# A recurrent and attention block on one core: a blocked inverse in four quadrants, and fewer small operations in differential attention

## The reference, cut to what matters

```
sa = S_{t-1} a_t
S_t = S_{t-1} diag(w_t) + sa b_t^T + v_t k_t^T ;  y_t = S_t r_t
```

## Time and profile before

| | us |
|---|---|
| median of 3 runs (lowest, highest) | 3494.92 (3494.77, 3496.0) |
| the profiled execution | 3495.8 |
| its span on the core | 3494.0 |
| PE busy | 3296.9 (94%) |
| DVE busy | 2061.9 (59%) |
| ACT busy | 1019.0 (29%) |
| POOL busy | 1679.5 (48%) |

### The profile page before, as it was taken

The page is one execution under the profiler, slowest core; times in us unless marked ns, Lnnn a source line. Parts: engine busy times, 40 slices in busy tenths (PEclk is TensorE's granted clock), DMA queues, the critical chain, the costliest instruction groups (busy, mean ns, idle before and its releaser), DMA issues.

```text
span 3494.0 us, 54483 instructions
## 1 busy us (share of the span) xinstructions
PE 3296.9 (94%) x20334; PEld 2615.5 (75%) x20334; DVE 2061.9 (59%) x2829; ACT 1019.0 (29%) x1866; POOL 1679.5 (48%) x1323
## 2 busy tenths in 40 slices
PE   7988999999999999989899899999989999999999
PEld 4766777777888888657778788887657677788887
DVE  4647777874566555541745575557551645576556
ACT  2152322222121112551435231113462435231112
POOL 3423222222657664225264566665326363666665
PEclk9999999999999999999999999999999999999999
DMA  5431111111323332112021233332102121223332
GB/s 204 166 123 45 38 32 38 31 38 43 115 70 96 96 97 72 37 43 91 31 89 53 83 92 96 96 97 67 54 25 91 49 79 49 85 85 97 94 94 95
DMA packets 71664, 268.48 MB, mean 77 GB/s; under 512 B 7840, under 2 KB 7968, under 8 KB 68384
## 3 DMA queue, kind: packets, MB, share of 16 engines
q1 hardware_dynamic: 69152, 260.73, 23.8%
q10 hardware_dynamic: 2304, 4.83, 0.4%
HBM read 263.44 MB, written 2.10 MB: 76 GB/s over the span
## 4 chain that ended last, share of the span: by engine, by line
PE 74%; DVE 19%; ACT 3%; issue 2%; DMA 1%; DVEq 0%; POOL 0%; SPq 0%; ACTq 0%; POOLq 0%
PE psum_a L574 10%; PE psum_a L577 10%; PE psum_a L578 10%; PE psum_d L574 5%; PE psum_d L577 4%; PE psum_d L578 4%; PE psum_d L637 4%; PE psum_d L1195 3%; PE psum_a L729 2%; PE psum_a L600 2%; PE psum_d L832 2%; PE psum_a L604 2%; PE psum_a L603 2%; DVE arena L2672 1%; PE psum_a L759 1%
## 5 line engine op out<-in xcount | busy, mean ns | idle before, releaser
L3274 POOL TENSOR_TENSOR w_lo<-raw,w_hi 128x1024 fp32r<-128x1024 f32 x440 | 1119.4, 2544 | 36.7
L3270 POOL TENSOR_TENSOR mark<-mark 128x1 f32<-128x1 f32 x438 | 105.5, 241 | 1738.4 <-PE psum_a L574 899.3
L574 PE MATMUL psum_a<-h_hi,w_hi 128*128 128x512 f32 x1712 | 675.2, 394 | 0.0
L577 PE MATMUL psum_a<-h_lo,w_hi 128*128 128x512 f32 x1712 | 667.4, 390 | 0.0
L578 PE MATMUL psum_a<-h_hi,w_lo 128*128 128x512 f32 x1712 | 667.4, 390 | 0.0
L3271 POOL TENSOR_SCALAR w_hi<-raw 128x1024 fp32r<-128x1024 f32 x440 | 471.2, 1071 | 33.7 <-DMA raw<-in_weights 33.7
L574 PEld LDWEIGHTS psum_a<-h_hi,w_hi 128*128 128x128 f32 x1712 | 322.1, 188 | 77.8 <-issue 11.2
L578 PEld LDWEIGHTS psum_a<-h_hi,w_lo 128*128 128x128 f32 x1712 | 322.0, 188 | 67.7
L577 PEld LDWEIGHTS psum_a<-h_lo,w_hi 128*128 128x128 f32 x1712 | 322.0, 188 | 67.4 <-issue 1.9
L574 PE MATMUL psum_d<-split,w_hi 128*128 128x512 f32 x848 | 331.2, 391 | 9.5 <-DVE x L3021 6.7
L577 PE MATMUL psum_d<-split,w_hi 128*128 128x512 f32 x848 | 330.0, 389 | 0.0
(11 more groups left out here) (393 smaller groups left out, 5775.5 us busy)
## 6 DMA issues: line engine op xcount, KB each, us to landing
raw<-in_weights SPq DMA_DIRECT2D x440, 512.0 KB, 3.6
plain<-in_ada SPq DMA_DIRECT2D x20, 1024.0 KB, 7.3
arena<-in_ada SPq DMA_DIRECT2D x4, 1024.0 KB, 17.4
x<-in_x SPq DMA_DIRECT2D x1, 2048.0 KB, 12.7
x<-in_x ACTq DMA_DIRECT2D x1, 2048.0 KB, 10.4
out<-x SPq DMA_DIRECT2D x8, 256.0 KB, 3.8
arena<-in_pe ACTq DMA_DIRECT2D x2, 512.0 KB, 3.6
const<-in_const ACTq DMA_DIRECT2D x1, 906.0 KB, 9.2
```

Of the source, the lines that this page charges most:

```text
L574: m = pe.eng.matmul(dst, wh, hi(t), start=t == 0, stop=False)
L577: pe.eng.matmul(dst, wh, lo(t), start=False, stop=False)
L3270: eng.tensor_tensor(b.mark[:, 1:2], b.mark[:, 0:1], b.mark[:, 0:1], ALU.add)
L3274: eng.tensor_tensor(lo, b.raw[:, s], hi.bitcast(F32), ALU.subtract).then_inc(sig["w_ready"], 1)
```

## The change

In the inverse, the third product and TC go. TN is transposed in each level by four PE transposes, which ACT copies to a new buffer, R_TW; the second product takes that. The first and second products (`products`) address all four pairs of row half and column half, where before two were used, and their results come in two banks by row half, 256 columns each, so that DVE's mask and its add are two operations of 256 columns each. The result of the first product lies swapped between halves, and the second swaps it back. After level 5 one more product with the identity (`diagonal`) gives the transposed blocks, which DVE copies to R_TF. R_TF holds the whole 128x128 transposed inverse, its unused quarter set to zero for j < 2, so `second` is one product of 128 rows for each head in place of two parts.

In the order: `second` stands ahead of the level's second product, on PE alone; `dve_rwkv_normed` stands ahead of level 1; the first maps of level 5 are made and masked behind that level's second product and its adds.

In differential attention the two negatives are one operation behind the second unit's maximum, so ACT waits once for a pair; the two reciprocals are one; and the sum of squares is taken by ACT, one step later.

```diff
         self.R_Z, self.R_TN = (ar(a).rearrange("p (u t) -> p u t", u=8) for a in (29, 30))
-        self.R_TC = [ar(a).rearrange("p (u t) -> p u t", u=8) for a in (31, 32)]
-        self.R_T6 = [ar(a).rearrange("p (u t) -> p u t", u=8) for a in (33, 34)]
+        self.R_TW = self.plain[:, 6].rearrange("p (u t) -> p u t", u=8)
+        self.R_TF = [ar(a, 2).rearrange("p (u t) -> p u t", u=8) for a in (31, 33)]
         self.R_E = (self.col[:, 156:159], self.col[:, 172:175])
...
         for r, u in self.heads(c):
-            pe.eng.matmul(tl.ps[upper, r], self.TC[upper, u], self.W[upper, r], start=True, stop=True)
-        for r, u in self.heads(c):
-            m = pe.eng.matmul(tl.ps[lower, r], self.T6[:, u], self.W[:, r], start=True, stop=True)
+            m = pe.eng.matmul(tl.ps[:, r], self.TF[:, u], self.W[:, r], start=True, stop=True)
         m.then_inc(tl.full, pe.up("full_a"))
         self.u = tl
...
 
-    def blocks(lhsT, rhs):
+    def products(lhsT, rhs):
+        tiles = [pe.tile("d") for _ in range(2)]
+        pe.eng.wait_ge(tiles[1].free, pe.emptied(tiles[1]))
+        for v in range(4):
+            for n, (row, out) in enumerate(((0, 0), (1, 1), (0, 1), (1, 0))):
+                m = pe.eng.matmul(tiles[row].ps[ROWS[out], v * HD:(v + 1) * HD], lhsT(v, row, out), rhs(v, row, out),
+                                  start=True, stop=True)
+                if v == 3 and n >= 2:
+                    m.then_inc(tiles[row].full, pe.up("full_d"))
+        return tiles[1]
+
+    def block(t, v, row, out):
+        return t[ROWS[row], 2 * v + out]
+
+    def diagonal(src):
         tl = pe.tile("d")
         pe.eng.wait_ge(tl.free, pe.emptied(tl))
         for u in range(8):
             for r in ROWS:
-                m = pe.eng.matmul(tl.ps[r, u * HD:(u + 1) * HD], lhsT(r, u), rhs[r, u], start=True, stop=True)
+                m = pe.eng.matmul(tl.ps[r, u * HD:(u + 1) * HD], src[r, u], b.ident[r, r], start=True, stop=True)
         m.then_inc(tl.full, pe.up("full_d"))
         return tl
...
+        inverse = pe_turned(pe, [b.R_TN[:, 2 * v:2 * v + 2].rearrange("p u t -> p (u t)") for v in range(4)])
         if c is not None:
             chain.first(c)
         if k == 2 and more:
...
+        if c is not None:
+            chain.second(c)
+        pe.eng.wait_ge(inverse.free, pe.taken(inverse))
+        pe.eng.wait_ge(z.free, pe.taken(z))
+        normal = products(lambda *at: block(b.R_TW, *at), lambda *at: block(b.R_Z, *at))
+        if k == 5:
             for src in (b.R_V, b.R_BH, b.R_KH):
                 turned = pe_turned(pe, [src[:, q * P:(q + 1) * P] for q in range(NQ)])
             pe_rwkv_maps(pe, j, (0, 1))
-        if k == 1:
-            pe.eng.wait_ge(pe.sem["t_ready"], pe.due("t_ready"))
-        pe.eng.wait_ge(z.free, pe.taken(z))
-        normal = blocks(lambda r, u: TC[r, u], b.R_Z)
-        if c is not None:
-            chain.second(c)
-        last = blocks(lambda r, u: b.R_Z[r, u], TC)
         if c is not None:
             chain.third(c)
...
+    last = diagonal(b.R_TN)
     maps = pe_rwkv_maps(pe, j, (2, 3))
     pe.eng.wait_ge(last.free, pe.taken(last))
     pe.eng.wait_ge(z.free, pe.taken(z))
-    last = corner(upper, lambda u: b.R_Z[lower, u], lambda u: b.R_T6[j % 2][lower, u])
+    last = corner(upper, lambda u: b.R_Z[lower, u], lambda u: TF[lower, u, HD:])
     if j:
         pe_rwkv_variance(pe)
...
         act_late_gate(a, 0)
-    for k in range(1, NQ + 1):
+    for k in range(1, NQ + 2):
+        a.eng.wait_ge(a.sem["full_a"], a.due("full_a"))
+        a.eng.wait_ge(a.sem[a.last], a.own())
+        a.eng.activation(b.R_TW, a.bank().rearrange("p (u t) -> p u t", u=8), ACT.Copy).then_inc(a.sem["free_a"], a.up("free_a"))
+        if k > NQ:
+            continue
         if j:
             act_rwkv_chunk(a, W)
...
-            a.eng.wait_ge(a.sem["s_ready"], a.due("s_ready"))
+            if s % 2:
+                a.eng.wait_ge(a.sem["s_ready"], a.due("s_ready"))
             if u.sink is not None:
                 a.eng.wait_ge(a.sem[a.last], a.own())
...
                     .then_inc(a.sem["free_a"], a.up("free_a"))
+        if 0 <= s - lag - 3 and units[s - lag - 3].v:
+            act_output_square(a, units[s - lag - 3])
+    for u in units[-2:]:
+        if u.v:
+            act_output_square(a, u)
+
+
+def act_output_square(a, u):
+
+    a.eng.wait_ge(a.sem["o_written"], a.due("o_written"))
+    a.eng.wait_ge(a.sem[a.last], a.own())
+    a.eng.activation(u.square[0], u.o, ACT.Square, accum_out=u.square[1]).then_inc(a.sem["act_step"], a.up("act_step"))
 
 
 def act_head_root(a, dst, rows, width, name):
...
+            u.two_top, u.two_inv = b.col[:, 119 + n % 4:121 + n % 4], b.col[:, n % 32 - 1:n % 32 + 1]
+            u.two_neg, u.two_sum = b.col[:, c - 2:c + 2:2], b.col[:, c - 1:c + 3:2]
     return units
 
...
     v.eng.tensor_tensor(b.R_TN, b.R_TN, eye, ALU.add).then_inc(v.sem["t_ready"], v.up("t_ready"))
-    for r in ROWS:
-        v.eng.wait_ge(v.sem[v.last], v.own())
-        v.eng.tensor_tensor(TC[r], b.R_LM[r, :, 0, r], low1t[r], ALU.mult).then_inc(v.sem["dve_step"], v.up("dve_step"))
-    v.eng.wait_ge(v.sem[v.last], v.own())
-    v.eng.tensor_tensor(TC, TC, eye, ALU.add).then_inc(v.sem["t_ready"], v.up("t_ready"))
+    if j >= 2:
+        dve_rwkv_normed(v, j - 2)
     for k in range(1, 6):
-        level = v.each(b.const[:, C_LEVEL + (k - 1) * HD:C_LEVEL + k * HD], 8)
-        v.eng.wait_ge(v.sem["full_d"], v.due("full_d"))
-        v.eng.wait_ge(v.sem[v.last], v.own())
-        v.eng.tensor_tensor(b.R_Z, eight(v.bank()), level, ALU.mult).then_inc(v.sem["free_d"], v.up("free_d"))
+        level = v.each(b.const[:, C_LEVEL + (k - 1) * HD:C_LEVEL + k * HD], 4)
+        for half in range(2):
+            v.eng.wait_ge(v.sem["full_d"], v.due("full_d"))
+            v.eng.wait_ge(v.sem[v.last], v.own())
+            v.eng.tensor_tensor(every(b.R_Z, half), four(v.bank()), level, ALU.mult).then_inc(v.sem["free_d"], v.up("free_d"))
         if k == 2 and more:
             dve_rwkv_input(v, j + 1, 2)
         if k == 2 and j >= 2:
-            dve_rwkv_normed(v, j - 2)
             dve_rwkv_mixed(v, j - 2)
         if k == 4 and more:
             for step in (4, 8, 9):
...
+            dst = every(b.R_TN, half)
             v.eng.wait_ge(v.sem["full_d"], v.due("full_d"))
             v.eng.wait_ge(v.sem[v.last], v.own())
-            v.eng.tensor_tensor(dst, dst, eight(v.bank()), ALU.add).then_inc(v.sem["free_d"], v.up("free_d"))
+            v.eng.tensor_tensor(dst, dst, four(v.bank()), ALU.add).then_inc(v.sem["free_d"], v.up("free_d"))
...
-                step = "free_d"
+            dve_rwkv_maps(v, (0, 1))
         if j and k < NQ:
             dve_rwkv_state(v, j - 1, k - 1)
         if k in (1, 3) and more:
             dve_rwkv_input(v, j + 1, k)
+    if j < 2:
+        v.eng.wait_ge(v.sem[v.last], v.own())
+        v.eng.memset(TF[HD:P, :, 0:HD], 0.0).then_inc(v.sem["dve_step"], v.up("dve_step"))
+    v.eng.wait_ge(v.sem["full_d"], v.due("full_d"))
+    ps, step = eight(v.bank()), "dve_step"
+    for r, cols in zip(ROWS, ROWS):
+        v.eng.wait_ge(v.sem[v.last], v.own())
+        v.eng.tensor_copy(TF[r, :, cols], ps[r]).then_inc(v.sem[step], v.up(step))
...
+        step = "free_d"
     dve_rwkv_maps(v, (2, 3))
     if more:
         dve_rwkv_input(v, j + 1, 7)
...
-                v.eng.tensor_scalar(u.neg, u.top, -1.0 if u.scale is None else -u.scale, None, ALU.mult)\
-                    .then_inc(v.sem["s_ready"], v.up("s_ready"))
-            else:
-                v.eng.tensor_scalar(u.neg, u.top, -1.0, u.scale, ALU.mult, ALU.mult)\
-                    .then_inc(v.sem["s_ready"], v.up("s_ready"))
-            if extra:
-                extra(s)
+            if s % 2:
+                v.eng.wait_ge(v.sem[v.last], v.own())
+                v.eng.tensor_scalar(u.two_neg, u.two_top, -u.scale, None, ALU.mult).then_inc(v.sem["s_ready"], v.up("s_ready"))
         if 0 <= s - 2 < len(us) and us[s - 2].ready == "p_ready" and us[s - 2].v:
             u0, u1 = us[s - 3], us[s - 2]
             if base + s - 1 > 0:
                 v.eng.wait_ge(v.sem["e_done"], v.value("e_done", base + s - 1))
             v.eng.wait_ge(v.sem[v.last], v.own())
-            v.eng.reciprocal(u0.inv, u0.sum).then_inc(v.sem["dve_step"], v.up("dve_step"))
-            v.eng.wait_ge(v.sem[v.last], v.own())
-            v.eng.reciprocal(u1.inv, u1.sum).then_inc(v.sem["dve_step"], v.up("dve_step"))
+            v.eng.reciprocal(u1.two_inv, u1.two_sum).then_inc(v.sem["dve_step"], v.up("dve_step"))
             v.eng.wait_ge(v.sem[v.last], v.own())
             v.eng.scalar_tensor_tensor(u1.inv, u1.inv, u1.neg_lam, u0.sum, ALU.mult, ALU.mult)\
                 .then_inc(v.sem["dve_step"], v.up("dve_step"))
@@ -2703,8 +2729,7 @@
                 v.eng.tensor_scalar(u.o, v.bank()[:, 0:u.width], us[s - lag - 2 - late_by].inv, None, ALU.mult)\
```

(3 more changed lines are left out.)

30 lines of the change are left out of this document (10 added, 20 removed).

## The result

The changed kernel takes 3465.64 us (median of 4 runs, 3464.59 to 3468.85), the kernel before beside it 3494.85 (3494.34 to 3496.0): ratio 0.9917, interval 0.9905 to 0.993. It is 29 us faster where I had forecast 63, and lies above my range, which ended at 3460. By the spans of the two profiled executions (3494.0 and 3463.4) the gain of 30.6 us is made of three sums of opposite sign, read from the starts of the same PE instructions in both traces: the recurrent stage with the chain behind it gains 45, differential attention *loses* 8.5 in two layers, and 6 are lost in small steps in stages that were not touched.

What follows compares the result with a forecast made beforehand. DVE was taken to set the mean pace, PE that of single pairs. Terms 37 + 10 - 4 + 7 + 3 + 1 + 9 = 63 us off 3494.9 gave 3432, range 3412 to 3452, widened to 3460.

Steps and rivals of the forecast that it cites:

- Four quadrants: Recurrent levels: first and second products run four wide, 0.69 us in place of 1.15, each saving 0.46 us.
- rival A: Recurrent levels: products run two wide as today, so 37 us stay, giving 3469 us; chance 0.06.
- Level 4: Level 4 saves 1.4 us in each of head pairs 1 to 6, less 4 in all for slow DVE operations.
- Level 5 and the end: End of head pairs 1 to 6: DVE 1.1 and PE 0.8 us earlier, taken as 1.0 a head pair.
- Head pair 7: Last head pair, without preparation: 1.2 to 1.85 us saved in four levels, 1.0 in the fifth, 7 in all.
- Head pair 0: First head pair, without a chain: shorter products against half operations save 3 us, with the clearing of R_TF.
- The normalization: That of head pair j - 2, moved ahead of level 1, is hidden there and saves 10 us of 12.1.
- Differential attention: Merged negative and reciprocal, squares on ACT: 4.6 us saved a layer, 9 for two.
- DVE sets the mean pace: Differential attention before the change: DVE takes 4.41 us a pair, 70.6 for sixteen; PE sets that of single pairs.
- I give back 1.5: Differential attention: 1.5 us deducted because ACT's exponential of the first unit now waits for the second's maximum.
- Rival C: Stalls in levels 1 and 3 bring PE to 1.2 GHz, doubling levels 2 and 4's dense products; about 3509; chance 0.04.
- Rival B: ACT's copies set the pace, losing 1 us more in each of 28 levels with a chain; 3460 us; chance 0.09.

Runs made afterwards that it cites:

- e4: Changed kernel with each product's 32 instructions issued as sixteen over one diagonal pair of quadrants, then sixteen over the other; 3479.7 us.
- e6: Changed kernel with POOL's subtraction for the weights' low part over 8 of 1024 columns, in all blocks but the first ones; 3368.9 us.
- e7: Kernel before the change with POOL's subtraction for the weights' low part cut to 8 of 1024 columns; 3394.1 us.
- e13: e6 with the two copies of the diagonal blocks at a head pair's end on ACT in place of DVE; 3356.7 us.
- e9: e2 with the normalization back behind level 2's mask in the last head pair (7) alone; 3449.7 us.
- e11: Kernel before the change with only the move of the normalization of head pair j - 2 ahead of level 1's mask; 3510.2 us, ratio 1.0041.
- e5: e2 with the normalization of head pair j - 2 back behind level 2's mask, where it stood before the change; 3481.4 us.
- e2: Changed kernel with one negative for each unit again in differential attention; one reciprocal a pair and squares on ACT stay; 3450.0 us, ratio 0.9872.
- e12: Changed kernel, merged negative kept, with ACT's copy of the transposes ahead of the exponential of the next pair's first unit; 3447.5 us, ratio 0.9862.
- e1: Changed kernel with differential attention as before the change, the recurrent stage keeping the whole change; 3450.9 us, ratio 0.9875.
- e3: Changed kernel with the sums of squares back on DVE, merged negative and reciprocal kept; 3473.1 us.

## Why the prediction was wrong, step by step

*Four quadrants:* right in the size (0.69 us) and that the products run four wide; rival A is out. That every 0.46 us arrives was too simple (e4), yet levels 1 to 3 came out as forecast: level 1 of head pairs 1 to 6 saved 7.0 us (forecast 7.5), levels 2 and 3 26.4 (forecast 25 with the move's 10). PE's stall ahead of `second` in level 1 is 0.66 (forecast 0.8), levels 2 plus 3 are 16.3 to 16.7 in head pairs 1 to 6 (forecast 16.3).

*Level 4:* the term "1.4, less 4 for slow operations" was 4.4 us for six head pairs and measured 1.2. The allowance was right: slowed operations take 7.1 us of the changed kernel's level 4 and 3.1 of that before (e6, e7), 4.0 more. The 1.4 was too much. Without the subtraction the level saves 5.3 us in six head pairs, 0.9 each in the mean: DVE, which ends it, ends at 10.1 and not at 9.8, and in two of them at 10.6 and 10.9.

*Level 5 and the end:* failed. "DVE 1.1 us and PE 0.8 us earlier at their ends" gave 6 us for six; measured 1.6. Without disturbance five of them gain 0.2 to 0.3 each, and head pair 1 loses 2.0, since I counted the clearing of R_TF in head pair 0 alone, although it stands for j < 2 (e6, e7). PE does reach the first corner 2.1 us earlier, but the way to the second grows from 2.6 to 4.4, where it waits for DVE's copies of the diagonal (e13).

*Head pair 7:* 7 forecast, 2.9 measured. I took the normalization as hidden there as elsewhere; behind an addition of 2.75 us it was not (e9: 3.0 us in level 1). My 1.8 us to spare were read in head pair 6, where nothing is slowed. *Head pair 0* came out (3.2 for 3), but by luck: without the subtraction it takes 6.7 us more than in the kernel before (e6, e7), and its level 2 takes 8.4 us in some kernels and 10.0 in others with the same work.

*The normalization:* right in the full change, for the reason given: the room comes from the dropped operations on TC (e11), without which only head pair 6 has enough of it. But I priced it as one term beside others; e5 and e11 show that its worth is anything from -15 to +31 us, by what stands around it.

*Differential attention:* this is the step that decides, +8.5 measured for -9, 17.5 of the 32 us missed by the spans. Two things failed in it. "DVE sets the mean pace" was wrong: of the fifteen intervals between the pairs' first products with v in the kernel before, nine are 5.2 to 5.8 us, and 5.2 to 5.5 in e2, with DVE's savings, so only the other six (20.6 us together) could shrink, and I had them at 6 x 2.58 = 15.5; e2 has them at 18.1. My 70.6 us for today also counted sixteen intervals of DVE where the 64 counted fifteen of PE. DVE's own pace came to 3.83 us where no gate stands (e12), not 3.65. And "I give back 1.5, because ACT's exponential of the first unit now waits" named the right wait and asked the wrong question. I priced the waiting instruction, not the queue behind it: the copy that PE waits for stood there (e2, e12). With the copy ahead the whole change takes 3447.5, inside my range, and the attention stretches gain 6.4 us in two layers. The table load behind the last square costs 1.0 a layer, for 0.5.

*The clock:* my sum had nothing for it. Rival C named a cost that is real and put it in the wrong place: with stalls of 0.66 us in level 1 the clock stays at 1.00 in levels 1 to 4 of head pair 1, but it is 0.54 behind a pause of 3.6 us (e5) and 0.85 behind one of 1.45 (e6), and the changed kernel has 16 us more at the low level than the one before. My sign "no lower than today" failed in head pair 1, 0.97 for 1.00. *Rival B* is out: level 1's stall is the one forecast.

The sum by the spans: 63 forecast, 30.6 measured; short by 17.5 in attention, 9 in the recurrent stage (3.2 level 4, 4.4 the ends, 4.1 head pair 7, less 2.7 won elsewhere), and 6 in untouched stages. The 6 go with the clock in amount and place: the 647 us behind the second differential attention, for one, take 646.8 to 647.1 in the four traces (before, e1, e3, e12) that have 14 us at the low level there, and 648.2 and 648.5 in the two (e2, changed) that have 17. That the clock alone makes them was not tested, and what lowers it in stages with the same work is open. Open too is why the first microseconds and head pair 0 differ by 1 to 2 us between kernels with the same work there.

## What to carry to other kernels

When a signal is merged for two users, follow the waiting engine's queue and ask what stands behind the wait: here one instruction fewer for a pair on DVE cost 15 us, and changing the order of two on ACT gave back 18. A move that "hides" an operation is worth what is free at its new place; price it with the rest of the change and without it, as the two can differ in sign. And a pause of PE can be paid twice, once as time and once as clock: here one of 3.6 us was followed by 3.4 us lost at the low level (e5).

## What was not expected of the hardware

DVE's tensor_tensor operations of 128x512 within the on-chip memory take 0.68 to 0.70 us in the changed kernel where POOL does nothing beside them (143 of them), and 0.89 to 2.87, 2.29 in the mean, where they meet POOL's subtraction alone (153). Beside the operation that makes the high part they take up to 1.57, even where the subtraction is nearly gone (e6). DVE's operations of 128x256 that read PSUM take 0.42 us in every trace. Without the subtraction (e6, e7) both kernels are 97 and 102 us faster, 26 and 39 of it in the recurrent stage. It is not that the weights come earlier, for PE waited only 2.8 us for POOL in either.

Cutting POOL's operation from 2.5 us into four of 0.84 shortens the slowed operations (1.28 us at most beside the subtraction alone) and helps by 10 us, though its total grows from 101 us (40 of 2.52) to 142 (175 of 0.84, four or five blocks more) in 550 us; eight of 0.52 raise it to 1709 us in the whole program, from 1114, and PE then waits for weights. Products ordered by pairs of quadrants still overlap where the pairs change (0.98 us for 32, against 1.15 on one pair and 0.69 on four in turn).
